# A convolution's input products with 512 moving columns for high and low activations together, in half units

## The reference

```python
def _causal_conv_silu(x, w):
    kw = w.shape[0]
    s = x.shape[1]
    xp = jnp.pad(x, ((0, 0), (kw - 1, 0), (0, 0)))
    y = sum(w[j].astype(jnp.float32) * xp[:, j:j + s] for j in range(kw))
    return jax.nn.silu(y)

def _hybrid_layer(h, norm_w, w_in, ...):
    u = _rmsnorm(h, norm_w)
    proj = jnp.matmul(u, w_in.astype(jnp.float32))
    ...
    qkv = _causal_conv_silu(dn_qkv, dn_conv_w)
    dq, dk_, dv_ = jnp.split(qkv, 3, axis=-1)
    dq = _l2norm(_heads(dq, DN_HEADS))
    dk_ = _l2norm(_heads(dk_, DN_HEADS))
    ...
    h_b = _gated_delta_chunkwise(dq, dk_, dv_, beta, g)
```

## Time and profile before

| | us |
|---|---|
| median of 3 executions | 1907.54 |
| lowest, highest | 1907.08, 1909.92 |
| the profiled execution | 1906.96 |
| its span | 1905.2 |

### The profile page before, as it was taken

How to read it: one execution, slowest core, us unless ns; L and a number is a source line. 1 busy time by engine, 2 the same in 40 slices (tenths; PEclk the granted TensorE clock), 3 DMA queues, 4 the chain that set the end, 5 groups by cost and what they waited for, 6 DMA issues and landing times.

```text
span 1905.2 us, 27734 instructions
## 1 busy us (share of the span) xinstructions
PE 1885.3 (99%) x10964; PEld 1635.8 (86%) x10964; DVE 1407.6 (74%) x2068; ACT 911.0 (48%) x1394; POOL 328.5 (17%) x550
## 2 busy tenths in 40 slices
PE   8999999999999999999999999999999999999998
PEld 8999999878888989888888888888888888888886
DVE  5786877767989788889989667666464676657675
ACT  6546455445433433434445465554444455544544
POOL 1034425161212222313223100000000000111000
PEclk9999999999999999999999999999999999999999
DMA  8555454546788787777888857655656543544563
GB/s 263 149 159 177 124 176 144 155 155 194 263 271 288 255 270 238 238 261 248 288 293 307 297 188 233 232 177 186 196 169 203 175 133 126 185 147 150 186 224 132
DMA packets 209745, 393.17 MB, mean 206 GB/s; under 512 B 13000, under 2 KB 62448, under 8 KB 208208
## 3 DMA queue, kind: packets, MB, share of 16 engines
q1 hardware_dynamic: 191248, 323.17, 52.0%
q0 software_dynamic: 18224, 68.17, 11.2%
q10 hardware_dynamic: 144, 0.07, 0.0%
HBM read 387.13 MB, written 4.23 MB: 205 GB/s over the span
## 4 chain that ended last, share of the span: by engine, by line
PE 92%; DVE 4%; POOL 1%; ACT 1%; issue 1%; DMA 0%; SPq 0%; DVEq 0%; ACTq 0%; POOLq 0%
PE GB L2188 50%; PE GB L2215 19%; PE GB L2200 9%; PE GB L2203 5%; PE SB L419 1%; PE SB L1759 1%; DVE WL L2112 1%; PE SB L1751 1%; POOL TB L1122 1%; POOL XB L1125 1%; PE SB L1858 1%; PE SB L1865 1%; PE SB L829 1%; PE SB L1216 1%; ACT WH L2107 0%
## 5 line engine op out<-in xcount | busy, mean ns | idle before, releaser
L2112 DVE TENSOR_TENSOR WL<-raw,WH 128x1024 fp32r<-128x1024 f32 x605 | 730.9, 1235 | 180.3 <-ACT WH L2107 179.1
L2107 ACT ACTIVATE WH<-raw 128x1024 fp32r<-128x1024 f32 x605 | 622.7, 1059 | 312.2 <-PE GB L2188 226.2
L2188 PE MATMUL GB<-WH,uHL 128*128 128x512 f32 x1792 | 484.6, 392 | 1.2 <-DVE WL L2112 1.2
L2188 PEld LDWEIGHTS GB<-WH,uHL 128*128 128x128 f32 x1792 | 333.2, 188 | 69.2 <-issue 1.3
L2215 PE MATMUL GB<-uHL,WH 128*128 128x256 f32 x2048 | 291.4, 285 | 1.6 <-DVE uHL L455 1.6
L2188 PE MATMUL GB<-WH,hHL 128*128 128x512 f32 x1024 | 279.4, 395 | 0.0
L2188 PE MATMUL GB<-WL,uHL 128*128 128x512 f32 x896 | 276.1, 389 | 0.0
L2215 PEld LDWEIGHTS GB<-uHL,WH 128*128 128x128 f32 x2048 | 264.0, 192 | 2.9 <-DVE uHL L455 1.8
L2188 PEld LDWEIGHTS GB<-WH,hHL 128*128 128x128 f32 x1024 | 190.6, 188 | 41.1 <-issue 2.7
L1446 DVE SCALAR_TENSOR_TENSOR macc<-wm,csil,macc 128x512 f32<-128x512 f32 x300 | 209.5, 748 | 2.7 <-DMA wm<-in_w_mod 1.5
L2188 PEld LDWEIGHTS GB<-WL,uHL 128*128 128x128 f32 x896 | 168.2, 188 | 35.5
(11 more groups left out here) (408 smaller groups left out, 1911.9 us busy)
## 6 DMA issues: line engine op xcount, KB each, us to landing
raw<-in_w_in SPq DMA_DIRECT2D x512, 512.0 KB, 4.5
raw<-in_w_out SPq DMA_DIRECT2D x96, 512.0 KB, 5.2
wm<-in_w_mod POOLq DMA_DIRECT2D x64, 512.0 KB, 5.5
wm<-in_w_mod POOLq DMA_DIRECT2D x64, 256.0 KB, 4.3
xin<-in_x SPq DMA_DIRECT2D x4, 512.0 KB, 5.8
E<-decay_rows POOLq DMA_DIRECT2D x4, 512.0 KB, 4.2
hres<-in_x POOLq DMA_DIRECT2D x1, 2048.0 KB, 10.7
cin<-in_ctx POOLq DMA_DIRECT2D x1, 2048.0 KB, 11.5
```

Of the source, the lines that this page charges most:

```text
L2107: e.activation(place(s)[0][:, :, :], raw[s % NR][:, :, :], ACT.Copy).then_inc(*wh.inc("WH", s))
L2112: e.tensor_tensor(low[:, :, :], raw[s % NR][:, :, :], f32(high[:, :, :]), sub).then_inc(*wl.inc("WL", s))
L2188: m = e.matmul(banks[j][:, :], x[:, c, 128 * j:128 * j + 128], w[:, k, :], start=i == 0 and k == 0 and n == 0, stop=i == 7 and k == 1 and ...
```

## The change

Units qkv 1 to 11 go over from mode "ch" to mode "two"; unit 0 stays. Their loads become 4 blocks of 256 columns instead of 2 of 512. A new SBUF buffer `zz` (4 blocks of 256) takes the joined result: after slots 3 and 7 of a unit ACT copies the two second halves into it and DVE adds the two first halves, and the convolution of units 1 to 11 reads zz where it read GB. From unit 2 on the copy also waits until the convolution before has read its blocks of zz. PE takes stages in the middle of such slots too. Since USES has 11 more entries, the later units sit on the other pair of banks than before.

```diff
-            t.append(Unit("qkv", 3 * n + kind, "w_in", 0, 8208 + 2048 * kind + 512 * n, "ch", "u"))
+            t.append(Unit("qkv", 3 * n + kind, "w_in", 0, 8208 + 2048 * kind + 512 * n, "two" if n + kind else "ch", "u"))
...
+        def convolved(r, j):
+            return zz[:, j, :] if r else half(GB[j // 2], j % 2)
+
+        def low_halves_act(e, r, h, banks):
+            if r > 1:
+                e.wait_ge(*cv_dve.at(f"{2 * h + 1}3", r - 1))
+            for j in range(2):
+                a = e.activation(zz[:, 2 * h + j, :], half(banks[j], 1), ACT.Copy)
+            a.then_inc(*z_act.inc(f"h{h}", r - 1))
+
+        def halves_added_dve(e, r, h, banks):
+            e.wait_ge(*z_act.at(f"h{h}", r - 1))
+            for j in range(2):
+                v = e.tensor_tensor(zz[:, 2 * h + j, :], half(banks[j], 0), zz[:, 2 * h + j, :], add)
+            v.then_inc(*z_dve.inc(f"h{h}", r - 1))
+
         def conv_act(e, r):
             n, kind = divmod(r, 3)
-            banks = GB[2 * (r % 2):2 * (r % 2) + 2]
             y, th = yth[:, 0], yth[:, 1]
-            e.wait_ge(*slot.at("mm", end("qkv", r)))
+            if r:
+                e.wait_ge(*z_dve.at("h1", r - 1))
+            else:
+                e.wait_ge(*slot.at("mm", end("qkv", r)))
...
-                a = e.activation(y[:, j, :], half(banks[j // 2], j % 2), ACT.Identity,
+                a = e.activation(y[:, j, :], convolved(r, j), ACT.Identity,
...
-                    e.scalar_tensor_tensor(out=y[:, j, sh:], in0=half(banks[j // 2], j % 2)[:, 0:256 - sh],
+                    e.scalar_tensor_tensor(out=y[:, j, sh:], in0=convolved(r, j)[:, 0:256 - sh],
...
             k, n = UNITS[u].kind, UNITS[u].n
+            if UNITS[u].mode == "two" and k == "qkv":
+                return [z_dve.at(f"h{h}", n - 1)]
...
             for k in range(4):
+                if k == 2:
+                    take_turns(stages, s - 0.5)
                 c = 4 * i + k
```

More of the change, by code:

```diff
@@ L313, in hybrid_program @@
                     [("W1", [128, 4, 128], F32), ("U1", [128, 4, 128], F32), ("R2", [128, 4, 128], F32),
-                     ("U2", [128, 4, 128], F32), ("NTd", [128, 8, 32], F32)],
+                     ("U2", [128, 4, 128], F32), ("NTd", [128, 8, 32], F32), ("zz", [128, 4, T], F32)],
                     [("wm0", [128, 2, 512], F32), ("wm1", [128, 2, 512], F32), ("macc", [128, 2, 512], F32),
@@ L328, in hybrid_program @@
         sq0 = R["sq0"]
+        zz = Z["zz"]
         W1, U1, R2, U2, NTd = (Z[n][:, :, :] for n in ("W1", "U1", "R2", "U2", "NTd"))
@@ L708, in condition_dve @@
             yield
+        z_act, z_dve = steps("z_act", "h0", "h1"), steps("z_dve", "h0", "h1")
         cv_act = steps("cv_act", "y", "t")
@@ L1554, in out_a_dve @@
         def out_a_dve(e, n):
-            banks = GB[2 * (n % 2):2 * (n % 2) + 2]
+            banks = pair(NUMBER["ya", n])
             s = slice(512 * n, 512 * n + 512)
@@ L1651, in hybrid_program @@
         KV = {(u.kind, u.n): k for k, u in enumerate(u for u in UNITS if u.kind in ("vaC", "vbC", "vaX", "vbX"))}
-        KS = {(u.kind, u.n): k for k, u in enumerate(u for u in UNITS if u.mode == "two")}
+        KS = {(u.kind, u.n): k for k, u in enumerate(u for u in UNITS if u.mode == "two" and u.kind != "qkv")}
         kc_to = {"kaC": kTaC, "vaC": vaC, "kbC": kTbC, "vbC": vbC, "kaX": kTaX, "vaX": vaX, "qa": qT2, "kbX": kTbX,
@@ L2168, in product_pe @@
             if unit.mode == "two":
-                m = halves_pe(e, unit, s, banks)
+                m = halves_pe(e, unit, s, banks, stages)
             elif unit.mode == "tok":
@@ L2191, in tokens_pe, with halves_pe @@
             return m
-        def halves_pe(e, unit, s, banks):
+        def halves_pe(e, unit, s, banks, stages):
             i = SLOTS[s][1] % 4
@@ L2225, in product_act @@
                 e.wait_ge(*slot.at("mm", s))
-                keys_act(e, k, n, i // 4, pair(u, i // 4))
+                (low_halves_act(e, n, i // 4, pair(u, i // 4)) if k == "qkv" else keys_act(e, k, n, i // 4, pair(u, i // 4)))
                 return
@@ L2254, in product_dve @@
             if UNITS[u].mode == "two" and i in (3, 7):
-                keys_dve(e, k, n, i // 4, pair(u, i // 4))
+                (halves_added_dve(e, n, i // 4, pair(u, i // 4)) if k == "qkv" else keys_dve(e, k, n, i // 4, pair(u, i // 4)))
                 return
```

## The result

| | before | after |
|---|---|---|
| median, us | 1908.03 (4 executions) | 1925.67 (4 executions) |
| lowest to highest | 1907.08 to 1909.92 | 1924.25 to 1926.33 |
| the profiled execution, its span | 1906.96, 1905.2 | 1925.95, 1924.2 |

The kernel before has one execution more here than in the table ahead of the prediction, so its median is 1908.03 and not 1907.54. The changed kernel takes 1.009 times as long (95% interval 1.0073 to 1.0108), 17.6 us more by the medians and 19.0 by the two profiled spans. The forecast was 1919.0, 11.5 us more, with a range of 1906 to 1928: the direction and the range held, the size was 6.7 us short.

The account below looks back on a forecast made before the run. PE, 92% of the chain, was taken as the bound, so its products' time and longer waits count. -8.4 + 5.65 + 1.7 + 0.65 + 0.3 + 1.5 + 10.1 = +11.5 on 1907.5: 1919.0 us, range 1906 to 1928.

Parts of the forecast that it names:

- The products: PE in the 88 slots of units 1 to 11: each slot 0.095 us shorter in mode two, -8.4 us.
- The estimate of 1.8 us: PE's products in units 1 to 11: the skill page's formula gives a gain of 1.8 us instead of 8.4.
- Slot 12: Unit 1's second half: PE stops until convolution 0 has read its last block from the banks, +5.65 us.
- The clock: Behind the stop at slot 12: PE falls to 1.2 GHz, +1.7 us (between 0 and 3.4).
- rival B: POOL's chains: DVE and POOL take turns throughout, 18 to 26 us, total 1927 to 1935; chance 0.11.
- Scores, U: PE's existing waits: scores +0.65 us in group 0, +0.3 in groups 1 and 2 together; U +1.5 in groups 0 and 1.
- POOL: GpSimd's substitution, groups 0 to 2: convolution's two SBUF inputs lengthen each chain 3.3 us, PE waits for X, +10.1 us.
- the sign: POOL's L1122 and L1125 beside the convolution's zz operations would take 0.5 to 0.7 us.
- What costs nothing: ACT's copies, DMA rows, bank alternation, zz's single buffer, and weight splits with at least 1.1 us of slack: no cost.
- a sign against it: The forecast is wrong if L2112's WL makes PE wait; then DVE pays, not POOL.

Follow-up runs that it names:

- the pair of experiments above: Kernel before plus ACT's copies to zz: convolution of units 1 to 11 with two SBUF inputs, 1915.93 us; with one SBUF and one PSUM input, 1908.11 us.
- the copies alone: Kernel before, all products in mode ch, but from unit 1 on ACT copies the product to zz and DVE's convolution reads zz: 1915.93 us.
- the kernel with two units: Changed kernel with only units 1 and 2 in mode two, unit 0 copied out, slot 15's copies behind the gates' work: 1912.02 us.
- unit0_copied: Changed kernel, but ACT also copies unit 0's product to zz and convolution 0 reads zz: 1919.36 us, ratio 1.0052.

## Right and wrong, step by step

**The products: right.** -8.1 us where -8.4 stood, 0.092 us a slot, as the two modes' rows had it. The estimate of 1.8 us by the Trainium skill (TensorE: Matmul & The Clock Gate, "Wait — 56ns, not 53.3ns?") was far off here; its formula leaves no room for the 120 ns that a product of 256 columns with a weight load of its own takes in these rows.

**Slot 12: right.** 5.65 us forecast, 5.52 waited and 5.7 by the slots. The count of what DVE has ahead of step 33 held piece by piece, and copying unit 0 out took away exactly that. DVE's time line in the changed kernel (additions, j2, WL of slot 15, j3; PE could have started slot 12 at 56.46):

```profile
57.34 0.76 DVE L746 TENSOR_TENSOR zz<-GB,zz 128x256 f32<-128x256 f32 x2 [1.93 <-ACT zz L740]
58.02 1.51 DVE L792 SCALAR_TENSOR_TENSOR yth<-GB,vcol,yth 128x255 f32<-128x255 f32 x3
59.44 1.21 DVE L2131 TENSOR_TENSOR WL<-raw,WH 128x1024 fp32r<-128x1024 f32 x1
60.57 1.51 DVE L792 SCALAR_TENSOR_TENSOR yth<-GB,vcol,yth 128x255 f32<-128x255 f32 x3
```

**The clock: the mechanism right, the number of times wrong.** The fall behind slot 12 was forecast at 1.7 us and cost 1.4. The other four were not in the sum; 8.5 us in all, the largest part of what was missing. The step that failed is the one that counted a fall at slot 12 alone and left those behind the other stops to rival B. 7.1 of the 8.5 us lie in those four.

**Scores, U: mis-sized.** Group 0's scores: +0.65 forecast, +3.1 measured. The step counted the additions inside the chain from colA on, which is right (from colA's start to the end of NT grew from 19.3 to 20.0 us), but took it that DVE comes to colA as early as before, since it had 2.30 us of idle time there. It comes 1.9 us later against PE: 1.9, 0.7 for the additions behind it and 0.5 for PE's gain are the 3.1. U: 1.5 forecast, 2.0 measured, because the convolution's operations are not faster from SBUF: a triple takes 1.51 us as before, the 0.055 us an operation were taken from operations of another kind.

**POOL: right in kind, half in size.** The second input in SBUF lengthens the chains of groups 0 to 2, not that of group 3, 2.6 to 3.0 us each against 3.3 forecast. The chain's length was near for the wrong reason: the forecast had one POOL operation a triple waiting, at 0.4 us; in the trace all three end with the DVE operation that they began beside, at 0.12 us each. That is how rival B had it (the engines take turns throughout), at a third of its price of 0.36 us. Operations of 0.5 to 0.7 us, which the prediction named as the sign, did not come either: two of each three take 0.39 to 0.46 and the first 0.24 to 0.37. The waits at L933 in groups 0 to 2 grew by 4.8 us rather than 10.1. In groups 0 and 2 it is 2.2 each: PE itself had been held up by WL of slots 40 and 88 (0.5) and the chain was shorter than assumed (0.7). In group 1 it is 0.5, because the clock had fallen in slot 65 and PE came 1.9 us later.

By the Trainium skill (SBUF — State Buffer, "Who interferes with whom") this contention needs two SBUF inputs on DVE and a GpSimd operation that reads SBUF; the pair of experiments above, 36.0 us of chain with two and 33.0 with one, agrees. So does the way in which POOL's operations end with DVE's.

**What costs nothing: not quite.** The splits in slots 24, 40, 64 and 88 were said to have 1.1 us of slack and to be given back what the additions take. They are 0.3 to 0.6 us late each, since the faster convolution that was to give it back does not exist, and PE's gain eats the slack. This is 2.0 us. The prediction named waits for WL as a sign against it, "then DVE pays, not POOL". DVE does not pay beside POOL: its convolution operations in the chains take 0.49 us on the mean for 0.48, and with the copies alone PE waits for no WL here. What makes the splits late is thus not the contention. At slot 24 it is the additions: cut to 8 columns, they let it come 1.05 us sooner. For the other three slots this is argued and not shown.

That the time lies in the range is in part luck, since the errors of the single terms partly cancelled: POOL's 5.3 us too much against 6.8 of clock (8.5 for 1.7), 2.5 of scores, 2.0 of splits and 1.2 of small things too little, which is the 7.2 us between the sums of 11.5 and 18.7.

## What to carry over

In this kernel a cheaper product on the engine that bounds it was worth its saving only where no other chain has less slack than the saving. Count the slack of every wait in the changed stretch, minus what the bounding engine gains by then. When an operand moves from PSUM to SBUF, look whether the operation then has two inputs in SBUF and what GpSimd does beside it. When a unit is cut in halves that rotate over the same buffers, the buffers come back after half the time: look at the last unit of the old kind, whose slow reader now holds up the second half, and copy that one out.

## What the hardware showed that I had not expected

POOL's operations of 0.24 us and DVE's of 0.48 with two SBUF inputs go in step, one for one, when both run in a chain; POOL's chain pays 0.12 us for each and DVE's operations 0.01.

The granted clock fell behind stops as short as 2.11 us (1.77 in the kernel with two units), and once behind no longer wait than 0.34 us: ahead of slot 65 PE had that wait for WL at 247.09, the value transposes at 245.7 and 16 products of one column at 250.2 (L816), and the clock was 0.50 from 252.8 to 256.2. The transposes and the products of one column run in the kernel before too, where no fall followed.

```profile
177.92 0.40 PE L2226 MATMUL GB<-uHL,WL 128*128 128x256 f32 x2
180.43 0.69 PE L933 MATMUL SB<-X,NT 32*32 32x32 f32 x32 [2.11 <-DVE X L1069]
181.05 1.17 PE L2223 MATMUL GB<-uHL,WH 128*128 128x512 f32 x2
```

Whether a given stop is followed by a fall changes from run to run: the same stop for X of group 0 in the unit0_copied kernel had none, and six of the twelve experiments' traces had one near the start (at about 15 us), where the kernels are alike, while the others, the kernel before and the changed one had none. So a difference of one or two us between two traces is first to be looked for in the clock. A new stop in this kernel cost, where a fall followed, 1.4 to 2.2 us more than its own length.

The convolution's operations on DVE take nearly the same time whether the first input is in PSUM or in SBUF, the second being in SBUF (0.48 and 0.49 us on the mean in POOL's chains, 1.51 for three in both).
